# Roots of summed rows by ScalarE and VectorE instead of GpSimd, and tile 0's transposes inside the last product

## The chip, the cores and the metric

The kernel runs on one core of one Trainium2 chip. The metric is device time in microseconds (us) of one launch, as the median of several. Five engines of the core have a part: TensorE (PE; its weight loads are PEld), VectorE (DVE), ScalarE (ACT), GpSimd (POOL) and SyncE (SP), which issues most transfers. Each works through its own list of instructions in order; semaphores tie the lists together.

## The reference

Two blocks of a transformer, 512 tokens of width 1024, all in float32. What matters here is the seam between the second block's first layer (a gated MLP) and its second (attention in a sliding window):

```python
def rms_norm_2(x, g):
    y = xf * lax.rsqrt(jnp.mean(xf * xf, axis=-1, keepdims=True) + EPS)   # EPS = 1e-6
    return (y * g).astype(x.dtype)
...
y = gmlp_mixer(rms_norm_2(h, a_pre_g), ...)     # ends in  y @ w_out, 2048 -> 1024
h = h + rms_norm_2(y, a_post_g)                 # root "a", one per token
kv_in = rms_norm_2(h, kv_norm_g)                # root "h3", one per token
k_shared = kv_in @ w_k;  v_shared = kv_in @ w_v
...
q, z = jnp.split(rms_norm_2(h, b_pre_g) @ b_w_in, 2, axis=-1)   # same root "h3"
```

## The kernel before

Tokens lie in four tiles of 128 partitions. Every product is made of three passes of `fp32r` matmuls: each operand is split into a rounded part (`whi`, `actB_hi`) and a remainder (`wlo`, `actB_lo`), and `exact` adds hi*hi, hi*lo and lo*hi. The order of PE's work is a list of blocks made by `tensor_order`, which PE follows strictly; the other engines have their order written out by hand.

The output product of the gated layer comes as fourteen units `("a", n)` of two blocks each, `("A", n, r)` for two halves of rows; a block has four steps k of three matmuls. `rows_by_half` waits before each step for the half of `wlo` that it reads (`w7_lo`), so steps 2 and 3 of unit 13 wait for the second half of `lo_a(13)`. ScalarE writes the unit's `whi` (`hi_a`, L1155) and VectorE its `wlo` (`lo_a`, L1743).

Then, for each tile of tokens t:
- VectorE adds up the product (`add_kept`, L1849), ScalarE squares each half with a sum along the row (`square_a`, L950), VectorE multiplies by the gain (`part_gain`, L1895);
- GpSimd takes the root (`root`: L795 adds the two sums and EPS into `ms`, L798 raises it to -0.5 into `rstd`);
- VectorE adds it to the residual in two halves (`h3_in`, L1903), ScalarE squares these (`h3_out`), GpSimd takes the root of h3;
- ScalarE scales the tile (`normed_n`, L1304), PE transposes it (`turn("n", t)`, L2173, eight transposes in two banks), ScalarE copies it out as `actB_hi` (`turned_n`, L961), VectorE takes the remainder `actB_lo` (`rest_n`, L1421);
- PE makes the new layer's values (`("v5", t)`: eight steps, waits for both remainders of the tile) and keys (`("Fa", "k5", 0)` for tiles 0 and 1, `("Fa", "k5", 1)`, `("F", "k5", f)` for the rest).

GpSimd meanwhile splits the weights of v5, k5 and q5 (`split_half`: two `whi` at L841, then two `wlo` at L850, for each half). For k5 it waits until PE is done with unit 12, and for its second half until ScalarE has scaled it by the norm's gain (`scale_two`, L1313); for q5 until PE is done with unit 13. The roots stand in this list at places written in `after`: those of "a" for tiles 0 and 1 stand between the last two `v5lo`, the others among k5's and q5's splits. All the four tiles' roots, "a" and "h3", make eight of two instructions each.

The last lines of PE's order around the seam, before:

```python
o += [("A", n, r) for n in (range(4), range(4, 14))[half] for r in range(2)]
o += turn("n", 0) + turn("n", 1) + [("v5", 0), ("v5", 1)]
o += [("Fa", "k5", 0)] + turn("n", 2) + [("Fa", "k5", 1)] + turn("n", 3)
```

Of the kernel before, what the change touches and what calls it, by code (L numbers as in the profile page):

```python
# [8 lines left out]
P = 128  # L9
# [143 lines left out]
LANDED = landings()  # L153
SQUARES_A = [(0, 0), (1, 0), (2, 1), (3, 1), (0, 1), (1, 1), (2, 0), (3, 0)]
# [33 lines left out]
def tensor_order():  # L188
# [42 lines left out]
    o += turn("n", 0) + turn("n", 1) + [("v5", 0), ("v5", 1)]  # L231
# [87 lines left out]
def program(nc, x, p, pre_norm_gain, w_in, lambda_q1, lambda_k1, lambda_q2, lambda_k2, subln_gain,  # L319
# [9 lines left out]
    with ctx:  # L329
# [40 lines left out]
        mhalf = sb("mhalf", [P, 1])  # L370
# [141 lines left out]
        ms_ready = sem("ms_ready")  # L512
        rstd_ready = {n: sem(f"rstd_{n}") for n in NORMS}
# [4 lines left out]
        pads_made = sem("pads_made")  # L518
# [10 lines left out]
        msq_attn, rstd_attn, attn_normed, attn_out = (sem("msq_attn"), sem("rstd_attn"),  # L529
# [241 lines left out]
        def _(pool):  # L771
            pool.memset(ident[:, :], 0.0).then_inc(consts_made, 1)
            pool.memset(mhalf[:, :], -0.5).then_inc(consts_made, 1)
            pool.memset(ones[:, :], 1.0).then_inc(consts_made, 1)
            pool.wait_ge(consts_made, 3)
# [24 lines left out]
            def root_attn(h):  # L800
                pool.wait_ge(attn_sq, 4 * h + 4)
                pool.tensor_scalar(ms_attn[:, h, :], ss_attn[:, h, :], 1.0 / DV1, SUBLN_EPS, ALU.mult, ALU.add)\
                    .then_inc(msq_attn, 1)
                pool.wait_ge(msq_attn, h + 1)
                pool.tensor_tensor(r_attn[:, h, :], ms_attn[:, h, :], mhalf[:, 0:1].to_broadcast([P, T]), ALU.pow)\
                    .then_inc(rstd_attn, 1)
# [111 lines left out]
            after[at("v5", 0, 1) - 0.25] = [lambda: root("a", 0, D), lambda: root("a", 1, D)]  # L918
            after[at("v5", 0, 1)] = [lambda: root("h3", 0, D)]
            after[at("k5", 0, 0) - 0.5] = [lambda: root("h3", 1, D)]  # L920
            after[at("k5", 0, 1) - 0.5] = [lambda: root("a", 2, D)]
            after[at("k5", 0, 1)] = [lambda: root("a", 3, D), lambda: root("h3", 2, D)]
            after[at("q5", 0, 0) - 0.5] = [lambda: root("h3", 3, D)]
# [11 lines left out]
        def _(act):  # L935
# [67 lines left out]
            def job_out(i):  # L1003
# [7 lines left out]
                if s == "c":  # L1011
                    act.wait_ge(pads_made, 1)
# [222 lines left out]

            def h3_out(t):
                for c in range(2):
                    act.wait_ge(h3_ready, 2 * t + c + 1)
                    square("h3", t, c, resid[:, t, c * HALF:(c + 1) * HALF])
# [67 lines left out]
            def scale_two(s, h):  # L1307
# [3 lines left out]
                for k in range(4):  # L1311
                    w = src[:, k * 256:(k + 1) * 256]
                    A(w, w, ACT.Copy, scale=kvg[:, 4 * h + k:4 * h + k + 1]).then_inc(w_scaled, 1)  # L1313
# [11 lines left out]
            square_a(1, 0)  # L1325
            hi_a(10)
# [19 lines left out]
            h3_out(2)  # L1346
            normed_n(2)
            v5_out(0)
            h3_out(3)
# [57 lines left out]
        def _(dve):  # L1407
# [28 lines left out]
            V.memset(gcv[:, :, 0:2], 0.0).then_inc(pads_made, 1)  # L1436

            dve.wait_ge(consts_made, 5)
# [4 lines left out]
            V.memset(base1[0:64, HALF - 64:HALF], MASKED).then_inc(base_step, 1)  # L1443

# [460 lines left out]

            def rest_n(t):
                for j in range(2):
                    rest("n", t, j)
# [41 lines left out]
            h3_in(3)  # L1950
            v5_rest(0)
# [118 lines left out]
        def _(pe):  # L2070
# [105 lines left out]
            def ready(b):  # L2176
# [48 lines left out]
                if kind == "v5":  # L2225
                    pe.wait_ge(lo["n"], 2 * (s + 1))
# [30 lines left out]
            def work(b):  # L2257
# [64 lines left out]
                if kind == "v5":  # L2322
# [4 lines left out]
                    for k in range(KD):  # L2327
                        H, L = halves_of(n, k // 2)
# [29 lines left out]
            pe.wait_ge(consts_made, 4)  # L2358
# [29 lines left out]
```

## Time and profile before

| | |
|---|---|
| median of three runs | 885.3 us (885.14 to 886.25) |
| the profiled execution | 885.75 us, its span 884.0 us |
| PE busy | 868.2 us (98%), 4220 matmuls |
| VectorE, ScalarE, GpSimd busy | 537.2, 360.3, 542.8 us |

The span is the time from the first to the last instruction of the profile; what is left of the execution's time lies around it. Busy times are sums over instructions of an engine. PE's come from modelled ends of pipelined matmuls, so that what counts is where its next start is late. In the timelines an instruction that has been issued and waits for another engine's access counts as running: a duration above the usual one of its kind is such a wait.

### The profile page before, as it was taken

What the parts mean: (1) busy time and instruction counts of PE and PEld (TensorE: products, weight loads), DVE (VectorE), ACT (ScalarE), POOL (GpSimd) and SP (SyncE); (2) the same over time, 40 slices, a digit from 0 to 9 for tenths busy, and PEclk for the clock granted to TensorE, in tenths of its full rate; (3) what the DMA queues carried; (4) which work ended last, traced back from release to release, by engine and by line L of the source; (5) the groups of instructions that cost most, each with busy time, mean ns of one, the idle gap of its engine ahead of it and who ended that gap; (6) DMA issues with size and microseconds to landing.
All of it is one profiled execution on the core that took longest, in us unless ns stands there. A gap on an engine that the chain in (4) does not pass through costs nothing.

```text
span 884.0 us, 11936 instructions
## 1 busy us (share of the span) xinstructions
PE 868.2 (98%) x4220; PEld 722.0 (82%) x4220; DVE 537.2 (61%) x880; ACT 360.3 (41%) x804; POOL 542.8 (61%) x604
## 2 busy tenths in 40 slices
PE   8999999999999999999999999999997999999997
PEld 6888888888888787888888888888887888888886
DVE  6125648875035489775765535556996457788624
ACT  4123333431134377546112321113775536767622
POOL 7766556587789832317975038771359798566352
PEclk9999999999999999999999999999999999999999
DMA  7533231342322468885742253526962222112202
GB/s 198 167 120 96 74 92 51 96 143 92 128 90 96 124 146 177 208 203 190 162 124 95 73 190 96 125 90 152 217 180 71 72 73 93 51 49 72 73 1 95
DMA packets 81517, 102.65 MB, mean 116 GB/s; under 512 B 11826, under 2 KB 54322, under 8 KB 81459
## 3 DMA queue, kind: packets, MB, share of 16 engines
q1 hardware_dynamic: 72752, 85.12, 30.1%
q0 software_dynamic: 8704, 16.78, 11.2%
q8 instruction: 34, 0.56, 0.3%
q14 instruction: 25, 0.20, 0.1%
q10 hardware_dynamic: 2, 0.00, 0.0%
HBM read 99.79 MB, written 2.10 MB: 115 GB/s over the span
## 4 chain that ended last, share of the span: by engine, by line
PE 88%; POOL 4%; DVE 2%; DMA 2%; ACT 2%; issue 1%; POOLq 0%; DVEq 0%; ACTq 0%
PE bank L2076 26%; PE bank L2078 26%; PE bank L2077 26%; PE bank L2319 2%; PE bank L2347 1%; PE bank L2173 1%; DMA gain<-in_a_w_in 1%; DVE wlo L1667 1%; POOL wlo L850 1%; PE bank L2292 1%; PE bank L2342 1%; PE bank L2341 1%; DMA raw<-in_a_w_in 1%; POOL ms L795 1%; POOL whi L841 1%
## 5 line engine op out<-in xcount | busy, mean ns | idle before, releaser
L850 POOL TENSOR_TENSOR wlo<-raw,whi 128x512 fp32r<-128x512 f32 x204 | 280.4, 1404 | 0.7 <-ACT whi L972 0.7
L841 POOL TENSOR_SCALAR whi<-raw 128x512 fp32r<-128x512 f32 x202 | 140.8, 733 | 188.1 <-PE bank L2078 179.1
L2076 PE MATMUL bank<-actB_hi,whi 128*128 128x512 f32 (+1 forms) x416 | 159.6, 384 | 0.6 <-POOL wlo L850 0.6
L2077 PE MATMUL bank<-actB_lo,whi 128*128 128x512 f32 (+1 forms) x416 | 158.7, 381 | 0.0
L2078 PE MATMUL bank<-actB_hi,wlo 128*128 128x512 f32 (+1 forms) x416 | 158.5, 381 | 0.0
L2076 PE MATMUL bank<-whi,actA_hi 128*128 128x512 f32 x318 | 125.9, 396 | 1.2 <-DVE actA_lo L1421 0.7
L2078 PE MATMUL bank<-whi,actA_lo 128*128 128x512 f32 x318 | 124.0, 390 | 0.0
L2077 PE MATMUL bank<-wlo,actA_hi 128*128 128x512 f32 x318 | 123.9, 390 | 0.0
L2076 PEld LDWEIGHTS bank<-actB_hi,whi 128*128 128x128 f32 x416 | 78.3, 188 | 15.4 <-issue 1.1
L2078 PEld LDWEIGHTS bank<-actB_hi,wlo 128*128 128x128 f32 x416 | 78.2, 188 | 15.2
L2077 PEld LDWEIGHTS bank<-actB_lo,whi 128*128 128x128 f32 x416 | 78.3, 188 | 14.1
L2076 PE MATMUL bank<-actA_hi,whi 128*128 128x512 f32 x224 | 87.9, 392 | 0.0
L2077 PE MATMUL bank<-actA_lo,whi 128*128 128x512 f32 x224 | 87.4, 390 | 0.0
L2078 PE MATMUL bank<-actA_hi,wlo 128*128 128x512 f32 x224 | 87.3, 390 | 0.0
L2076 PEld LDWEIGHTS bank<-whi,actA_hi 128*128 128x128 f32 x318 | 59.7, 188 | 15.3 <-issue 1.9
L2078 PEld LDWEIGHTS bank<-whi,actA_lo 128*128 128x128 f32 x318 | 59.7, 188 | 12.6
L2077 PEld LDWEIGHTS bank<-wlo,actA_hi 128*128 128x128 f32 x318 | 59.8, 188 | 12.0 <-issue 0.2
L2076 PE MATMUL bank<-whi,actB_hi 128*128 128x512 f32 x144 | 56.5, 393 | 0.2 <-DVE wlo L1667 0.2
L2078 PE MATMUL bank<-whi,actB_lo 128*128 128x512 f32 x144 | 56.1, 390 | 0.0
L2077 PE MATMUL bank<-wlo,actB_hi 128*128 128x512 f32 x144 | 56.0, 389 | 0.0
L1776 DVE TENSOR_TENSOR acc<-acc,gcv 128x512 f32<-128x512 f32 x16 | 15.6, 974 | 58.3 <-ACT gcv L1228 58.3
L2078 PEld LDWEIGHTS bank<-actA_hi,wlo 128*128 128x128 f32 x224 | 42.1, 188 | 8.9
(269 smaller groups left out, 1579.4 us busy)
## 6 DMA issues: line engine op xcount, KB each, us to landing
raw<-in_a_w_in SPq DMA_DIRECT2D x44, 512.0 KB, 4.2
raw<-in_w_in SPq DMA_DIRECT2D x32, 512.0 KB, 3.9
raw<-in_b_w_in SPq DMA_DIRECT2D x16, 512.0 KB, 3.4
raw<-in_a_w_out SPq DMA_DIRECT2D x12, 512.0 KB, 3.3
gain<-in_a_w_out POOLq DMA_DIRECT2D x9, 512.0 KB, 8.2
raw<-in_w_out SPq DMA_DIRECT2D x8, 512.0 KB, 3.4
raw<-in_w_ple_gate SPq DMA_DIRECT2D x8, 512.0 KB, 3.3
gain<-in_a_w_in POOLq DMA_DIRECT2D x8, 512.0 KB, 7.7
```

Source lines behind the costliest of these rows:

```text
L795: pool.tensor_scalar(m, ss[:, n, t, 0:1], ss[:, n, t, 1:2], EPS, ALU.add, ALU.add).then_inc(ms_ready, 1)
L841: pool.tensor_scalar(H, src[:, i * HALF:(i + 1) * HALF], 1.0, 1.0, ALU.mult, ALU.mult).then_inc(w_hi, 1)
L850: ins = pool.tensor_tensor(L, src[:, i * HALF:(i + 1) * HALF], H.bitcast(f32), ALU.subtract)
L1667: V.tensor_tensor(L, src, H.bitcast(f32), ALU.subtract).then_inc(w7_lo, 1)
L1776: V.tensor_tensor(acc[:, f % 2, :], acc[:, f % 2, :], gcv[:, f % 2, 0:S], ALU.mult).then_inc(zu_made, 1)
L2076: M(out_, whi_, xhi_, start=start, stop=False)
L2077: M(out_, whi_, xlo_, start=False, stop=False)
L2078: return M(out_, wlo_, xhi_, start=False, stop=stop)
L2173: ins = nc.tensor.transpose(bank[:, k * P:(k + 1) * P], src, ident[:, :])
L2292: ins = M(bank[:, qt * P:(qt + 1) * P], wgtT1[:, k * P:(k + 1) * P], tile(vtok, k)[:, h * P:(h + 1) * P], start=k == 0, stop=k == qt)
L2319: ins = M(bank[:, n * P:(n + 1) * P], big[:, n, f * P:(f + 1) * P], wcT[:, (f // 2) * P:(f // 2 + 1) * P], start=True, stop=True)
L2341: M(out_, q, khi(g)[:, keys], start=True, stop=False)
```

## The change

1. The eight roots leave GpSimd. ScalarE now squares at a scale of 1/64 instead of 1/32, so that the sums are a quarter of the mean square. It adds a quarter of EPS to the first sum (`add_eps`, into `ms`) and takes the root of the sum of both (`std`, `Sqrt`, into `rstd`); this is half of the root mean square, with the table's error.
2. VectorE (`inverse`) makes one step of Heron of it and its reciprocal: four instructions on one column.
3. Tile 0's transposes stand ahead of the last block of the last product, `("A", 13, 1)`.
4. The first half of a v5 block waits for the first remainder of its tile only.
5. The lists of ScalarE and VectorE around the seam are rewritten. VectorE has tile 0's inverse and `h3_in(0)` ahead of the second half of `lo_a(13)`. ScalarE scales the second half of k5 in two parts, the second behind the squares of h3 of tile 0. A `Sqrt` of one column stands behind `square_a(1, 0)`, so that the table is loaded there.
6. Two semaphores are merged into others (`pads_made`, `msq_attn`), and GpSimd has one more memset at the start.

```diff
-    o += turn("n", 0) + turn("n", 1) + [("v5", 0), ("v5", 1)]
+    assert o.pop() == ("A", 13, 1)
+    o += turn("n", 0) + [("A", 13, 1)] + turn("n", 1) + [("v5", 0), ("v5", 1)]
...
+            pool.memset(eps[:, :], EPS / 4).then_inc(consts_made, 1)
             pool.memset(ones[:, :], 1.0).then_inc(consts_made, 1)
-            pool.wait_ge(consts_made, 3)
+            pool.wait_ge(consts_made, 4)
...
-            after[at("v5", 0, 1) - 0.25] = [lambda: root("a", 0, D), lambda: root("a", 1, D)]
-            after[at("v5", 0, 1)] = [lambda: root("h3", 0, D)]
-            after[at("k5", 0, 0) - 0.5] = [lambda: root("h3", 1, D)]
-            after[at("k5", 0, 1) - 0.5] = [lambda: root("a", 2, D)]
-            after[at("k5", 0, 1)] = [lambda: root("a", 3, D), lambda: root("h3", 2, D)]
-            after[at("q5", 0, 0) - 0.5] = [lambda: root("h3", 3, D)]
...
-                A(junk[:, :], src, ACT.Square, scale=1.0 / 32, accum_out=ss[:, NORMS[name], t, c:c + 1])\
+                A(junk[:, :], src, ACT.Square, scale=1.0 / 64 if name in BY_ROOT else 1.0 / 32,
+                  accum_out=ss[:, NORMS[name], t, c:c + 1])\
...
+            def add_eps(name, t, tiles, c, done):
+                n = NORMS[name]
+                act.wait_ge(squared[name], done)
+                A(ms[:, n, t:t + tiles], ss[:, n, t:t + tiles, c], ACT.Identity, bias=eps[:, 0:1]).then_inc(std_step, 1)
+            def std(name, t, c, done):
+                n = NORMS[name]
+                act.wait_ge(std_step, STD_STEP["eps", name, t // 2 * 2 if name == "a" else t])
+                act.wait_ge(squared[name], done)
+                A(rstd[:, n, t:t + 1], ss[:, n, t, c:c + 1], ACT.Sqrt, bias=ms[:, n, t:t + 1]).then_inc(std_step, 1)
...
             square_a(1, 0)
+            act.wait_ge(consts_made, 6)
+            A(lams[:, 7:8], eps[:, 0:1], ACT.Sqrt)
...
             hi_a(13)
+            add_eps("a", 0, 2, 0, 2)
             square_a(0, 1)
+            std("a", 0, 1, 5)
             square_a(1, 1)
-            scale_two("k5", 1)
+            std("a", 1, 1, 6)
+            scale_two("k5", 1, (0, 1))
+            add_eps("a", 2, 2, 1, 4)
             h3_out(0)
+            scale_two("k5", 1, (2, 3))
+            normed_n(0)
             h3_out(1)
-            normed_n(0)
+            turned("n", 0, 0)
             normed_n(1)
-            turned_n(0)
+            turned("n", 0, 1)
             square_a(2, 0)
+            std("a", 2, 0, 7)
             turned_n(1)
             square_a(3, 0)
+            std("a", 3, 0, 8)
             h3_out(2)
+            h3_square(3, 0)
             normed_n(2)
             v5_out(0)
-            h3_out(3)
+            h3_square(3, 1)
+            h3_std(3)
             v5_out(1)
             normed_n(3)
...
+            def inverse(name, t):
+                n, c = NORMS[name], ROOTED_LAST[name, t]
+                nth = 3 * next(inverses)
+                last, mean, first, sum_ = (ss[:, n, t, k:k + 1] for k in (c, 1 - c, 2, 3))
+                root = rstd[:, n, t:t + 1]
+                dve.wait_ge(std_step, STD_STEP[name, t])
+                V.tensor_tensor(mean, last, ms[:, n, t:t + 1], ALU.add).then_inc(root_step, 1)
+                V.reciprocal(first, root).then_inc(root_step, 1)
+                dve.wait_ge(root_step, nth + 2)
+                V.scalar_tensor_tensor(sum_, mean, first, root, ALU.mult, ALU.add).then_inc(root_step, 1)
+                dve.wait_ge(root_step, nth + 3)
+                V.reciprocal(root, sum_).then_inc(rstd_ready[name], 1)
...
             lo_a(13, (0,))
             part_gain(0, 1)
+            inverse("a", 0)
+            h3_in(0)
             lo_a(13, (1,))
             part_gain(1, 1)
-            h3_in(0)
+            inverse("a", 1)
+            inverse("h3", 0)
             h3_in(1)
             add_kept(6, 0, p03_kept(0), a_out_(2, 0), (c7_made, 28 + 6))
+            inverse("h3", 1)
+            rest("n", 0, 0)
+            rest("n", 0, 1)
             add_kept(6, 1, p03_kept(1), a_out_(3, 0), (c7_made, 28 + 10))
-            rest_n(0)
             part_gain(2, 0)
-            rest_n(1)
+            inverse("a", 2)
+            rest("n", 1, 0)
             h3_in(2)
+            rest("n", 1, 1)
             part_gain(3, 0)
+            inverse("a", 3)
+            inverse("h3", 2)
             h3_in(3)
+            inverse("h3", 3)
...
-                    pe.wait_ge(lo["n"], 2 * (s + 1))
+                    pe.wait_ge(lo["n"], 2 * s + 1)
...
                     for k in range(KD):
+                        if k == 4:
+                            pe.wait_ge(lo["n"], 2 * t + 2)
```

## Rows read from the trace of the kernel before

**Rows 1.** The page's chain; busy us (count) by engine, granted clock, DMA, one stretch.
```profile
PE 88%; POOL 4%; DVE 2%; DMA 2%; ACT 2%; issue 1%; POOLq 0%; DVEq 0%; ACTq 0%
...
666.74:688.00 21.26, 15.93 (x128) 14.96 (x128) 11.59 (x17) 13.34 (x28) 20.27 (x29) 1.00 0.06 21
```

**Rows 2.** PE's waits, 640 to 712 us: total, times, longest.
```profile
PE bank L2173 <- ACT big L1304: 4.0, 4, 1.7
...
PE bank L2076 <- issue: 1.4, 2, 0.7
```

**Rows 3.** PE's timeline: start, us, line, operation [idle before, what ended it].
```profile
662.49 0.39 PE L2076 MATMUL bank<-whi,actA_hi 128*128 128x512 f32 x1
...
666.35 0.39 PE L2078 MATMUL bank<-whi,actA_lo 128*128 128x512 f32 x1
...
668.46 1.06 PE L2173 MATMUL bank<-ident,big 128*128 128x128 f32 x8 [1.72 <-ACT big L1304]
...
670.33 1.07 PE L2173 MATMUL bank<-ident,big 128*128 128x128 f32 x8 [0.81 <-ACT big L1304]
...
672.09 0.36 PE L2076 MATMUL bank<-v5hi,actB_hi 128*128 128x256 f32 x1 [0.69 <-issue]
...
682.15 1.06 PE L2173 MATMUL bank<-ident,big 128*128 128x128 f32 x8 [1.25 <-ACT big L1304]
...
688.07 0.36 PE L2076 MATMUL bank<-v5hi,actB_hi 128*128 128x256 f32 x1 [0.70 <-issue]
...
711.24 0.47 PE L2076 MATMUL bank<-actB_hi,whi 128*128 128x512 f32 x1 [0.59 <-POOL wlo L850]
```

**Rows 4.** ScalarE's timeline, 639 to 668 us.
```profile
639.57 1.06 ACT L1155 ACTIVATE whi<-raw 128x1024 fp32r<-128x1024 f32 x1 [2.00 <-PE bank L2078]
...
662.85 0.63 ACT L950 ACTIVATE junk<-resid 128x512 f32<-128x512 f32 x1 [1.65 <-DVE resid L1903]
...
667.18 1.13 ACT L1304 ACTIVATE big<-resid,rstd 128x1024 f32<-128x1024 f32 x1
```

**Rows 5.** The timelines of VectorE, then of GpSimd (POOL), 654 to 666 us.
```profile
655.90 1.09 DVE L1895 TENSOR_TENSOR big<-big,gain 128x512 f32<-128x512 f32 x1
...
658.11 1.70 DVE L1743 TENSOR_TENSOR wlo<-raw,whi 128x1024 fp32r<-128x1024 f32 x1
...
659.74 0.68 DVE L1895 TENSOR_TENSOR big<-big,gain 128x512 f32<-128x512 f32 x1
...
660.34 1.21 DVE L1743 TENSOR_TENSOR wlo<-raw,whi 128x1024 fp32r<-128x1024 f32 x1
...
662.08 0.74 DVE L1903 SCALAR_TENSOR_TENSOR resid<-big,rstd,resid 128x512 f32<-128x512 f32 x1
...
663.92 1.78 DVE L1903 SCALAR_TENSOR_TENSOR resid<-big,rstd,resid 128x512 f32<-128x512 f32 x1 [0.44 <-POOL rstd L798]
...
654.77 1.69 POOL L841 TENSOR_SCALAR v5hi<-raw 128x512 fp32r<-128x512 f32 x1 [1.01 <-ACT raw L1313]
...
657.44 1.29 POOL L850 TENSOR_TENSOR v5lo<-raw,v5hi 128x512 fp32r<-128x512 f32 x1
...
658.89 1.62 POOL L795 TENSOR_SCALAR ms<-ss 128x1 f32<-128x1 f32 x1 [0.16 <-ACT junk L950]
...
663.87 1.29 POOL L850 TENSOR_TENSOR v5lo<-raw,v5hi 128x512 fp32r<-128x512 f32 x1
```

**Rows 6.** By line: least/median/most ns of one, first and last start, forms.
```profile
L1983 DVE TENSOR_TENSOR den<-rs,esk x16: 144/162/1250, 717.8 to 834.8; 128x4 f32<-128x4 f32 x16
...
L1395 ACT ACTIVATE esk<-den x16: 187/188/190, 717.5 to 834.6; 128x4 f32<-128x4 f32 x16
...
L1358 ACT ACT_TABLE_LOAD  x1: 1283/1283/1283, 702.2 to 702.2; - x1
...
L841 POOL TENSOR_SCALAR whi<-tok x4: 610/614/1043, 666.8 to 672.0; 128x512 fp32r<-128x512 f32 x4
...
L1421 DVE TENSOR_TENSOR actB_lo<-bank,actB_hi x16: 674/681/691, 320.4 to 688.5; 128x512 fp32r<-128x512 f32 x16
```

More of the change, by code:

```diff
@@ L153 @@
 LANDED = landings()
+STD_STEP = {step: n + 1 for n, step in enumerate(
+    [("eps", "a", 0), ("a", 0), ("a", 1), ("eps", "a", 2), ("eps", "h3", 0), ("h3", 0), ("eps", "h3", 1), ("h3", 1),
+     ("a", 2), ("a", 3), ("eps", "h3", 2), ("h3", 2), ("eps", "h3", 3), ("h3", 3)])}
+ROOTED_LAST = {("a", t): int(t < 2) for t in range(4)} | {("h3", t): 1 for t in range(4)}
 SQUARES_A = [(0, 0), (1, 0), (2, 1), (3, 1), (0, 1), (1, 1), (2, 0), (3, 0)]
@@ L369, in program @@
         rstd = sb("rstd", [P, 8, T])
-        mhalf = sb("mhalf", [P, 1])
+        mhalf, eps = sb("mhalf", [P, 1]), sb("eps", [P, 1])
         prob3 = sb("prob3", [P, D])
@@ L512, in program @@
         ms_ready = sem("ms_ready")
+        std_step, root_step = sem("std_step"), sem("root_step")
+        BY_ROOT = ("a", "h3")
         rstd_ready = {n: sem(f"rstd_{n}") for n in NORMS}
@@ L517, in program @@
         consts_made, ws_masked = sem("consts_made"), sem("ws_masked")
-        pads_made = sem("pads_made")
         base_step, lam_step, lam_exp, cols_scaled = (sem("base_step"), sem("lam_step"), sem("lam_exp"),
@@ L528, in program @@
         wt_copied, attn_copied, attn_sq = sem("wt_copied"), sem("attn_copied"), sem("attn_sq")
-        msq_attn, rstd_attn, attn_normed, attn_out = (sem("msq_attn"), sem("rstd_attn"),
+        rstd_attn, attn_normed, attn_out = (sem("rstd_attn"),
                                                       sem("attn_normed"), sem("attn_out"))
@@ L802, in root_attn @@
                 pool.tensor_scalar(ms_attn[:, h, :], ss_attn[:, h, :], 1.0 / DV1, SUBLN_EPS, ALU.mult, ALU.add)\
-                    .then_inc(msq_attn, 1)
-                pool.wait_ge(msq_attn, h + 1)
+                    .then_inc(ms_ready, 1)
+                pool.wait_ge(ms_ready, next(roots))
                 pool.tensor_tensor(r_attn[:, h, :], ms_attn[:, h, :], mhalf[:, 0:1].to_broadcast([P, T]), ALU.pow)\
@@ L1011, in job_out @@
                 if s == "c":
-                    act.wait_ge(pads_made, 1)
+                    act.wait_ge(base_step, 4)
                     if f >= 2:
@@ L1234, in square_a, with h3_square, h3_std @@
                 square("a", t, c, a_out_(t, c))
+            def add_eps(name, t, tiles, c, done):
[7 more added lines that the diff above has]
+                A(rstd[:, n, t:t + 1], ss[:, n, t, c:c + 1], ACT.Sqrt, bias=ms[:, n, t:t + 1]).then_inc(std_step, 1)
+            def h3_square(t, c):
+                act.wait_ge(h3_ready, 2 * t + c + 1)
+                square("h3", t, c, resid[:, t, c * HALF:(c + 1) * HALF])
+            def h3_std(t):
+                add_eps("h3", t, 1, 0, 2 * t + 1)
+                std("h3", t, 1, 2 * t + 2)
             def h3_out(t):
-                for c in range(2):
-                    act.wait_ge(h3_ready, 2 * t + c + 1)
-                    square("h3", t, c, resid[:, t, c * HALF:(c + 1) * HALF])
+                h3_square(t, 0)
+                h3_square(t, 1)
+                h3_std(t)
             def y4_hi(j):
@@ L1305, in normed_n, with scale_two @@
                   scale=rstd[:, NORMS["h3"], t:t + 1]).then_inc(tok_ready["n"], 1)
-            def scale_two(s, h):
+            def scale_two(s, h, cols=range(4)):
                 src, landed, value = raw_of(UNIT_NO[s, 0], h)
@@ L1310, in scale_two @@
                 act.wait_ge(small_in, 16 * 13)
-                for k in range(4):
+                for k in cols:
                     w = src[:, k * 256:(k + 1) * 256]
@@ L1434, in normed @@
                 ins.then_inc(tok_ready[turn], 1)
-            V.memset(gcv[:, :, 0:2], 0.0).then_inc(pads_made, 1)
-            dve.wait_ge(consts_made, 5)
+            dve.wait_ge(consts_made, 6)
             V.tensor_copy(base1, iot).then_inc(base_step, 1)
@@ L1443, in _ @@
             V.memset(base1[0:64, HALF - 64:HALF], MASKED).then_inc(base_step, 1)
+            V.memset(gcv[:, :, 0:2], 0.0).then_inc(base_step, 1)
             def square_x(t):
@@ L1904, in h3_in @@
                                            resid[:, t, half], ALU.mult, ALU.add).then_inc(h3_ready, 1)
+            inverses = count(0)
+            def inverse(name, t):
[10 more added lines that the diff above has]
+                V.reciprocal(root, sum_).then_inc(rstd_ready[name], 1)
             def rest_n(t):
@@ L2356, in work @@
                     return ins
-            pe.wait_ge(consts_made, 4)
+            pe.wait_ge(consts_made, 5)
             for b in ORDER:
```

## The prediction

> **What bounds the kernel now.** I read the page first: PE carries 88% of the chain that ended last, and nothing else more than 4% [rows 1], so the change can only take away time in which PE stands still, or make more of it. The table of stretches then shows where: from 666.74, where the gated layer's last product ends, to 688.00 PE is busy 15.93 of 21.26 us, at a granted clock of 1.00 [rows 1]. PE's waits over this stretch are 4.0 us for ScalarE's normed tiles, in four, and 1.4 that the list puts down to issue, in two [rows 2]. PE's timeline places them [rows 3]: the last product's last matmul starts at 666.35 and takes 0.39; tile 0's transposes start at 668.46 (1.72 idle), tile 1's at 670.33 (0.81), the first v5 product at 672.09 (0.69: it waits for VectorE's second remainder of tile 0), tile 2's transposes at 682.15 (1.25), the third v5 block at 688.07 (0.70, in the same way). With the little that is left at tile 3 that is the 5.3 us of the stretch, 0.6% of the span, and all that the change can win.
>
> **What makes the tiles late.** I read the other engines' timelines beside each other [rows 4, 5]. In the kernel before, GpSimd's root of tile 0's sum begins at 658.89 and needs 1.62 us for its first step, on one column, because VectorE works on two operands in SBUF in the meantime. That is the pattern of the whole stretch: such a VectorE instruction and a GpSimd one never overlap, and when both queue they alternate. VectorE's wlo at 658.11 takes 1.70 instead of 1.21, behind GpSimd's v5lo, which ends at 658.73. GpSimd's v5hi at 654.77 takes 1.69 instead of 0.61, behind a wlo, and VectorE's product at 655.90, issued behind that, takes 1.09 instead of 0.68. A half of h3 takes 1.78 instead of 0.74 beside a v5lo of 1.29 [rows 5, 6]. VectorE instructions with one operand in PSUM (the remainders, 0.68) keep their time.
>
> **Part by part.**
> Removed from GpSimd: eight roots of two instructions. The two of tiles 0 and 1 stood between the two v5lo and pushed the second one from 658.7 to 663.87 [rows 5]. Without them it is queued at 658.7, and k5's four instructions (two whi of 0.61, two wlo of 1.29) follow as soon as PE is done with unit 12, at 661.3: from unit 13's third step at 662.49 to its last matmul at 666.35 there are 17 pitches of 0.227 [rows 3], so its first step starts six pitches ahead of 662.49, at 661.1, and unit 12's last matmul ends 0.16 behind that. GpSimd's load is the same; it comes earlier, into the stretch where VectorE has its dependent work.
>
> Added to ScalarE: six additions and eight roots of one column. The nearest row is an exponential of 128x4, 0.19 [rows 6]; the next larger one, a square of 128x512, is 0.63 [rows 4], so each lies between 0.1 (overlapped) and 0.63, and I take 0.2. One load of the table, 1.28 [rows 6], plus 0.2 goes into ScalarE's idle 2.00 us before 639.57 [rows 4]: nothing. Were that idle time missing it would delay whi of the tenth unit by 1.5.
>
> Added to VectorE: 8 x 4 instructions of one column. The nearest row is 0.16 each [rows 6]; with 0.2 from one to the next that depends on it, a root costs 0.7. Two of the four (the sum, and the Heron step) have two operands in SBUF. Their price is the disputed term. The row of a 128x4 sum of two SBUF tiles has 144, 162 and 1250 ns as least, median and most, so a small one can wait for a whole GpSimd instruction: 0 to 1.1 more each. I let them wait.
>
> Moved: tile 0's eight transposes (0.9) ahead of the last block of the last product, and on VectorE the root and both halves of h3 of tile 0 ahead of the second half of wlo of the last unit. PE needs that half from 662.49, in the middle of the block before the transposes [rows 3]; before, it was there at 661.55 [rows 5]. A wait there stops everything behind it on PE.
>
> The start: one more memset of one column on GpSimd, below 0.1, ahead of an ident that PE has until the gain lands. I cost it at nothing.
>
> **The sum, walked through.** VectorE: first half of wlo ends 659.8, as before. GpSimd's second v5lo then runs to 661.0; the product with the gain, issued at 659.74, ends 661.5 (before: 660.42). Tile 0's inverse takes to 662.3. Its first half of h3 ends 663.2; GpSimd's first k5 wlo runs to 664.4; the second half ends 665.0; the second k5 wlo runs to 666.15; only then does wlo's second half run, to 667.2. PE waits for it from 662.5 to 667.3: **4.8 us**. PE ends that block (6 matmuls, pitch 0.227) at 668.7.
> ScalarE has the root of tile 0's h3 at 666.2 and then lets k5's second half go (at 667.0), so that GpSimd has two whi and two wlo from 667.7 to 671.4. VectorE's gain product, tile 1's inverse and tile 0's second inverse fall among them and end at 671.6 (without waits of the small ones: 669.0). The normed tile takes 1.14 [rows 4]: 672.8. Transposes start at 672.9 instead of behind the product: **4.2 us idle**. They end at 673.8, the last block (2.7) at 676.5, tile 1's transposes at 677.6. There the first v5 block starts, against 672.09: 5.5 us late.
> The rest: v5's second block wants tile 1's second remainder, which now stands behind tile 2's h3 on VectorE, and waits 2.6 in two places; tile 2's transposes wait 2.9, since all the small ones and h3 of tiles 2 and 3 run among GpSimd's q5 work. The third v5 block starts at about 696.3, against 688.07: **+8.2 us**. Behind it PE is bound by itself until 711.24, and its 0.59 there is GpSimd working from PE's own release, so it shifts along. The walk has three places where two engines ask within 0.1 us; won the other way they give back up to 1.6. So 6.6 to 8.6, middle **7.5**.
> The profiled execution took 885.75, its span 884.0 and 1.75 around it; it would become 893.3. The median of the runs is 885.3, 0.45 less: 892.8.
> The same bookkeeping, applied to the kernel before, gives tile 0's normed tile at 668.4 (trace: 668.31) and PE's transposes of tile 2 at 682.3 (682.15). That is why I trust its waits.
>
> A rule that bears on the disputed term: the Trainium skill, "SBUF — State Buffer", section "Who interferes with whom", says that a VectorE instruction with two SBUF inputs and a GpSimd instruction that reads SBUF exclude each other for the whole instruction, whichever came first. It makes no exception for small ones. The trace agrees for the large (1.78 against 0.74) and, in its maximum, for the small. By the page the small ones pay, which is the sum above; without it they might not, which is the first rival.
>
> **Rivals.**
> *Small sums slip through.* Only the large instructions alternate with GpSimd. For it: the median of 162 ns; against it: the maximum of 1250. PE still waits 4.8 at the last unit's second half, then 1.6 for tile 0 and 1.8 for tile 1, but the tail is short (1.4 in v5's second block, 0.4 at tile 2): the third v5 block at about 691.2, +3.0 us, 888.3.
> *The engines miss each other; faster.* If GpSimd's instructions fall into VectorE's pauses, VectorE goes through undelayed: wlo's second half at 663.1 (PE waits 0.7), tile 0's normed tile at 666.1 (1.6), 0.2 at tile 1, 0.4 in v5's second block, nothing at tiles 2 and 3. That is 2.9 idle instead of 5.3, 2.4 less; with the v5 blocks started on the first half of a tile the walk comes to 3.8 less. So 881.5 to 882.9, say 882.3. For it: this is what one gets by adding durations alone, and one collision decides much: if the second v5lo waits behind h3 rather than ahead of the gain product, VectorE gets its 1.25 back. It decides when wlo's second half ends before about 664.3. Against it: every time the two queued in the rows, they alternated.
> *A wash.* Half of the collisions: 885.3, within 0.2%.
> *PE loses its clock.* The granted clock is 1.00 in the stretch [rows 1], but no idle there exceeds 1.72; a wait of 4.8 has no row. If the level fell from 2.4 to 1.2 GHz behind it, each us of matmuls at that level would cost another. I put this into the upper end. The Trainium skill, "TensorE: Matmul & The Clock Gate", section "What's actually happening", says that an idle PE falls to the lower level; no row of this trace shows it.
> *The square is not in the root's table.* Then each of 8 roots would cost two loads of 1.28 on ScalarE, some 20 us, most of it on the path: 900 or more. Against it: the trace loads a table three times in all (the row of one is in [rows 6]), though squares, copies, tanh, gelu and exponentials mix.
>
> **How the numbers follow.** Full collisions 0.45; large ones only 0.23; faster 0.20; wash 0.09; tables 0.03. The range 883.5 to 895.0 takes in the middle cases and leaves out most of the faster one and the tables, about 2 in 10. 0.2% (1.8 us) is about what a measurement of this kernel can tell from no change. Faster 0.20, same 0.09, slower 0.71. The likeliest case alone: 891.9 to 893.9.
>
> **What would show it.** Right: a wait of PE on VectorE's wlo inside the last unit's first block, 4 us or more; the second v5lo straight behind the first; h3's halves at 0.74 and 1.8 in turn; small VectorE sums above 1 us at times; tile 0's transposes after 670. Wrong: wlo's second half done by 664; GpSimd idle while VectorE is busy; or a granted clock below 1.00, or tables loaded more than four times.

## The result and the profile after

| | before | after |
|---|---|---|
| median of the runs | 885.78 us (885.14 to 886.25, 5 runs) | 892.84 us (892.36 to 894.29, 5 runs) |
| the profiled execution, its span | 885.75, 884.0 us | 892.84, 891.1 us |
| PE busy | 868.2 us | 871.4 us |
| VectorE, ScalarE, GpSimd busy | 537.2, 360.3, 542.8 us | 550.3, 365.8, 536.2 us |

The changed kernel is slower: ratio 1.0085, 95% interval 1.007 to 1.010. The forecast was 892.8. The time is the one predicted, but not all of the steps are, as the parts below show.

The page's chain, and PE's waits from 640 to 722 us (total, times, longest) in the changed kernel. They answer to [rows 1, 2]:

```profile
PE 89%; DVE 6%; issue 1%; POOL 1%; ACT 1%; DMA 1%; DVEq 0%; POOLq 0%; ACTq 0%
```

```profile
PE bank L2138 <- DVE wlo L1779: 4.5, 1, 4.5
PE bank L2235 <- ACT big L1329: 4.2, 2, 2.7
PE bank L2138 <- DVE actB_lo L1458: 0.8, 1, 0.8
PE bank L2138 <- POOL wlo L859: 0.6, 1, 0.6
PE bank L2138 <- issue: 0.3, 1, 0.3
```

VectorE's part of the chain went from 2% to 6%, and a wait of 4.5 us on `wlo` (L1779, the line that was L1743) is new. PE's timeline places the waits (start, us, line, operation, idle before; L2138 to L2140 are the matmuls, L2235 the transposes):

```profile
661.76 0.39 PE L2140 MATMUL bank<-whi,actA_lo 128*128 128x512 f32 x1
666.63 0.80 PE L2138 MATMUL bank<-whi,actA_hi 128*128 128x512 f32 x1 [4.48 <-DVE wlo L1779]
667.22 0.63 PE L2139 MATMUL bank<-wlo,actA_hi 128*128 128x512 f32 x1
667.65 0.63 PE L2140 MATMUL bank<-whi,actA_lo 128*128 128x512 f32 x1
...
672.25 1.94 PE L2235 MATMUL bank<-ident,big 128*128 128x128 f32 x8 [2.69 <-ACT big L1329]
673.84 0.78 PE L2138 MATMUL bank<-whi,actA_hi 128*128 128x512 f32 x1
...
677.80 1.04 PE L2235 MATMUL bank<-ident,big 128*128 128x128 f32 x8
678.59 0.37 PE L2138 MATMUL bank<-v5hi,actB_hi 128*128 128x256 f32 x1
...
684.36 0.39 PE L2138 MATMUL bank<-v5hi,actB_hi 128*128 128x256 f32 x1 [0.76 <-DVE actB_lo L1458]
...
690.44 1.06 PE L2235 MATMUL bank<-ident,big 128*128 128x128 f32 x8 [1.51 <-ACT big L1329]
...
695.01 0.36 PE L2138 MATMUL bank<-v5hi,actB_hi 128*128 128x256 f32 x1
```

Two things are to be seen. First, PE stands still twice, for 4.48 and 2.69 us, where the kernel before had 1.72 and 0.81 [rows 3]. Second, the matmul at 667.65 starts 0.43 behind the one at 667.22; ahead of the wait that distance was 0.23. The stretches say why (busy us and count by engine, then the granted clock, DMA share, GB/s):

```profile
661.00:666.00 5.00, 1.15 (x6) 0.61 (x4) 4.91 (x5) 2.29 (x8) 4.49 (x4) 1.00 0.18 62
666.00:671.00 5.00, 2.93 (x6) 1.83 (x6) 4.86 (x11) 0.48 (x3) 4.48 (x5) 0.50 0.65 213
671.00:676.00 5.00, 3.75 (x13) 3.40 (x14) 3.39 (x8) 4.61 (x10) 2.39 (x4) 0.50 0.29 102
676.00:681.00 5.00, 5.00 (x36) 4.55 (x36) 3.66 (x6) 3.33 (x9) 2.88 (x4) 0.98 0.00 0
```

Behind the wait of 4.48 us the granted clock is 0.50, that is 1.2 GHz instead of 2.4, for about ten us (666 to 676), while VectorE is busy for 4.86 of 5.00 us and PE for 2.93.

Where the time went is read best from starts, counted from the place of the wait, unit 13's third step. The matmul ahead of it starts at 661.76, so that step would have started at 661.99; in the kernel before it started at 662.49.

| start, us from the third step's place | before | after | later by |
|---|---|---|---|
| the third step itself | 0 | 4.64 | 4.6 |
| tile 0's transposes | 5.97 | 10.26 | 4.3 |
| first v5 product | 9.60 | 16.60 | 7.0 |
| tile 2's transposes | 19.66 | 28.45 | 8.8 |
| third v5 block | 25.58 | 33.02 | 7.4 |

These 7.4 us are the loss in this stretch. The place itself stands 0.5 us earlier in the changed kernel's trace, so the third v5 block starts 6.9 later on the clock of the trace; the two profiled executions differ by 7.1.

VectorE's timeline shows what PE waited for, and GpSimd's what was beside it:

```profile
657.42 1.71 DVE L1779 TENSOR_TENSOR wlo<-raw,whi 128x1024 fp32r<-128x1024 f32 x1
659.06 1.78 DVE L1931 TENSOR_TENSOR big<-big,gain 128x512 f32<-128x512 f32 x1
...
661.81 2.56 DVE L1939 SCALAR_TENSOR_TENSOR resid<-big,rstd,resid 128x512 f32<-128x512 f32 x2
664.29 2.28 DVE L1779 TENSOR_TENSOR wlo<-raw,whi 128x1024 fp32r<-128x1024 f32 x1
...
668.36 1.15 DVE L1951 TENSOR_TENSOR ss<-ss,ms 128x1 f32<-128x1 f32 x1
...
669.61 1.11 DVE L1954 SCALAR_TENSOR_TENSOR ss<-ss,rstd 128x1 f32<-128x1 f32 x1
```

```profile
656.75 3.54 POOL L859 TENSOR_TENSOR v5lo<-raw,v5hi 128x512 fp32r<-128x512 f32 x2
660.95 1.20 POOL L850 TENSOR_SCALAR whi<-tok 128x512 fp32r<-128x512 f32 x2 [0.66 <-PE bank L2140]
662.12 3.37 POOL L859 TENSOR_TENSOR wlo<-tok,whi 128x512 fp32r<-128x512 f32 x2
```

The second `v5lo` stands straight behind the first (x2, 3.54 us), where two roots and 5.1 us stood between them before [rows 5]. So the product with the gain takes 1.78 where it took 0.68, and the second half of `wlo` 2.28 where it took 1.21. Two sums of one column take 1.15 and 1.11 us.

### The profile page after: what moved, and what is told of

The parts are those of the page before. It is cut to its first block, busy times and chain, and to the rows that moved or that the text cites. A ratio compares the mean times of both kernels' runs of the same rounds, so it can differ in the third digit from the quotient of the medians.

```text
span 891.1 us, 11978 instructions
## 1 busy us (share of the span) xinstructions
PE 871.4 (98%) x4220; PEld 724.5 (81%) x4220; DVE 550.3 (62%) x912; ACT 365.8 (41%) x820; POOL 536.2 (60%) x589
## 4 chain that ended last, share of the span: by engine, by line
PE 89%; DVE 6%; issue 1%; POOL 1%; ACT 1%; DMA 1%; DVEq 0%; POOLq 0%; ACTq 0%
PE bank L2138 27%; PE bank L2139 26%; PE bank L2140 26%; PE bank L2235 2%; PE bank L2381 2%; PE bank L2411 1%; PE bank L2354 1%; PE bank L2406 1%; DVE wlo L1779 1%; PE bank L2405 1%; DVE wlo L1703 1%; DMA raw<-in_a_w_in 1%; DVE big L1931 1%; DVE resid L1939 1%; PE bank L2345 1%
## 5 line engine op out<-in xcount | busy, mean ns | idle before, releaser
L2138 PE MATMUL bank<-actB_hi,whi 128*128 128x512 f32 (+1 forms) x416 | 159.6, 384 | 0.6 <-POOL wlo L859 0.6
L2140 PE MATMUL bank<-actB_hi,wlo 128*128 128x512 f32 (+1 forms) x416 | 158.5, 381 | 0.0
L2138 PE MATMUL bank<-whi,actA_hi 128*128 128x512 f32 x318 | 126.9, 399 | 5.4 <-DVE wlo L1779 4.5
L2140 PE MATMUL bank<-whi,actA_lo 128*128 128x512 f32 x318 | 124.7, 392 | 0.0
L2138 PEld LDWEIGHTS bank<-actB_hi,whi 128*128 128x128 f32 x416 | 78.3, 188 | 15.5 <-issue 1.0
L2140 PEld LDWEIGHTS bank<-actB_hi,wlo 128*128 128x128 f32 x416 | 78.2, 188 | 15.3
L2138 PE MATMUL bank<-actA_hi,whi 128*128 128x512 f32 x224 | 87.9, 392 | 0.0
L2140 PE MATMUL bank<-actA_hi,wlo 128*128 128x512 f32 x224 | 87.3, 390 | 0.0
L2138 PEld LDWEIGHTS bank<-whi,actA_hi 128*128 128x128 f32 x318 | 60.3, 190 | 19.5 <-DVE wlo L1779 4.9
L2140 PEld LDWEIGHTS bank<-whi,actA_lo 128*128 128x128 f32 x318 | 60.3, 189 | 12.8
L2138 PE MATMUL bank<-whi,actB_hi 128*128 128x512 f32 x144 | 56.5, 393 | 0.2 <-DVE wlo L1703 0.2
L2140 PE MATMUL bank<-whi,actB_lo 128*128 128x512 f32 x144 | 56.1, 390 | 0.0
L2140 PEld LDWEIGHTS bank<-actA_hi,wlo 128*128 128x128 f32 x224 | 42.0, 188 | 8.8
```

What stands on the lines that cost most here:

```text
L2138: M(out_, whi_, xhi_, start=start, stop=False)
L2140: return M(out_, wlo_, xhi_, start=False, stop=stop)
```

## The experiments

All were timed against the kernel before on their own chip; its medians there were 885.7 to 885.8.

A median holds more than this stretch. The place of unit 13's third step is at 661.99 us in the trace of the changed kernel and at 663.74 in that of the second experiment's kernel, which differs from it in nothing ahead of 660 us; by so much single executions differ ahead of the seam. So each trace is also read by its stretch, the time from that place to the start of the third v5 block: 25.6 us in the kernel before, 33.0 in the changed one.

### The halves of wlo first

```diff
-            inverse("a", 0)
-            h3_in(0)
-            lo_a(13, (1,))
+            lo_a(13, (1,))
+            inverse("a", 0)
+            h3_in(0)
```

> The changed kernel with one line moved: VectorE makes the second half of wlo of the last unit ahead of tile 0's inverse and h3, as the kernel before does. My theory (the time lies in VectorE and GpSimd taking turns, and the order only decides where PE meets it): PE's wait of 4.5 us in the last unit's first block goes down to about 0.2, but tile 0's transposes then wait 6 us or more, since the chain of tile 0 gets that instruction ahead of it instead; the total falls by about 1, to 892 us. Rival (the order is the cause): the 4.5 us are won, with the lost clock behind them 6 or more: 886 to 888 us.

Measured: 891.87 us (891.3 to 894.18), ratio 1.0074, interval 1.0059 to 1.0089. The stretch is 31.2. The wait on `wlo` is gone, and where the changed kernel waits 4.48 and then 2.69 us, this one waits once, at the next place:

```profile
670.61 1.94 PE L2235 MATMUL bank<-ident,big 128*128 128x128 f32 x8 [6.12 <-ACT big L1329]
```

The order on VectorE places the wait and doesn't make it: what is short is VectorE's time up to tile 0's normed rows. The theory held: it had 892 us and 6 us or more at this place.

### The two sums in another form of instruction

```diff
-                V.tensor_tensor(mean, last, ms[:, n, t:t + 1], ALU.add).then_inc(root_step, 1)
+                V.tensor_scalar(mean, last, ms[:, n, t:t + 1], None, ALU.add).then_inc(root_step, 1)
...
-                V.scalar_tensor_tensor(sum_, mean, first, root, ALU.mult, ALU.add).then_inc(root_step, 1)
+                V.tensor_scalar(sum_, mean, first, root, ALU.mult, ALU.add).then_inc(root_step, 1)
```

The second and third operands are here scalars read through a pointer, one for each partition, and no longer tensors. The arithmetic is the same.

> The changed kernel with the two small VectorE instructions of each inverse that read two tensors in SBUF written as instructions that read one tensor and take the other operands as scalars of the partition; the arithmetic is the same. My theory (a small instruction waits for GpSimd's because of its second tensor operand): they stay at 0.15 to 0.2 us each, PE's first wait stays near 4.5, tile 0's normed tile comes about 2.5 us sooner, and the waits at tiles 1 and 2 and in the second v5 block shrink; 3 to 5 us less in all, 888 to 890 us. Rival (every VectorE instruction can be held, or the scalar operands are read in the same way): they still show 0.5 to 1.2 us, and the time stays at 892 to 893.

Measured: 890.22 us (889.77 to 891.03), ratio 1.0052, interval 1.0037 to 1.0067; the stretch is 29.5. The two lines by group (total us, mean ns), first in the changed kernel, then here:

```profile
L1954 DVE SCALAR_TENSOR_TENSOR ss<-ss,rstd 128x1 f32<-128x1 f32 x8 | 4.5, 558 | 0.3
...
L1951 DVE TENSOR_TENSOR ss<-ss,ms 128x1 f32<-128x1 f32 x8 | 3.5, 432 | 2.4 <-ACT rstd L1251 2.4
```

```profile
L1954 DVE TENSOR_SCALAR ss<-ss,rstd 128x1 f32<-128x1 f32 x8 | 2.2, 273 | 0.3
...
L1951 DVE TENSOR_SCALAR ss<-ss,ms 128x1 f32<-128x1 f32 x8 | 1.6, 203 | 2.2 <-ACT rstd L1251 2.2
```

In the new form none of the sixteen waits (the longest of each line took 0.22 and 0.28 us); PE's waits for normed tiles fell from 4.2 to 1.9 us, the one on `wlo` stayed at 4.5, and so did the lower clock behind it (0.55 in 666 to 671). So the small sums are worth 2.6 of the 7.1 us, by the stretch 3.5 of 7.4. The mechanism held; the median is just above the 888 to 890 that I expected.

### GpSimd held back

GpSimd waits, ahead of its second `v5lo`, until tile 0's second root is there:

```diff
+            after.setdefault(at("v5", 0, 1) - 0.25, []).append(lambda: pool.wait_ge(rstd_ready["h3"], 1))
```

> The changed kernel with GpSimd held: its second v5lo, and all that stands behind it, waits until tile 0's root of h3 is done. Nothing else differs. My theory (GpSimd's work having moved ahead into VectorE's dependent stretch is the cause): PE's first wait falls from 4.5 to about 1.2 us, tile 0's normed tile is there at about 666.0 instead of 672.1, the clock stays at 1.00, and the total falls by 3.5 to 5.5 us, to 887.5 to 889.5, though GpSimd's work now meets tiles 1 and 2. Rival (the added instructions on VectorE and ScalarE are themselves the cost): the first wait stays above 3 us and the time within 1 of 892.8, or longer for GpSimd's being late.

Measured: 889.98 us (889.69 to 891.44), ratio 1.0051, interval 1.0036 to 1.0066, just above the expectation; the stretch is 29.0. The wait on `wlo` falls to 0.75 and the clock stays at 1.00; tile 0's sums take 0.15 and 0.22.

```profile
663.82 0.50 PE L2139 MATMUL bank<-whi,actA_hi 128*128 128x512 f32 x1 [0.75 <-DVE wlo L1780]
```

```profile
679.92 1.25 DVE L1952 TENSOR_TENSOR ss<-ss,ms 128x1 f32<-128x1 f32 x1
```

But the collisions move on: tile 1 has small sums of 1.03 and 1.12 us, tile 3 of 1.25, 1.14 and 1.24, and PE waits 6.9 us for normed tiles, in four. GpSimd's early work on v5 and k5 makes the first wait; the small sums are a second cause by themselves.

### The clock kept up

Matmuls that no one reads (`ones` by `ident`, into a free bank) stand where PE waits: 36 ahead of the third step of unit 13, 20 ahead of tile 0's transposes.

```diff
+            def fill(count):
+                pe.wait_ge(c7_made, 28 + 14)
+                for _ in range(count):
+                    M(psum[7][:, 0:P], ident[:, :], ones[:, :], start=True, stop=True)
...
+                    if (n, r, k) == (13, 0, 2):
+                        fill(36)
...
+                        if (name, t, j) == ("n", 0, 0):
+                            fill(20)
```

> The changed kernel with 36 small matmuls into a free bank in the place where PE waits for the second half of wlo, and 20 more where it waits for tile 0's normed tile; they take less time than the waits. It asks what the lower granted clock costs, 0.50 from 666 to 676 us in the changed kernel. My theory: the clock stays at 1.00, the transposes take 1.06 instead of 1.94 and the last product's matmuls come 0.23 apart instead of 0.43; of the 3.3 us of slow work 1.2 lie in the second wait anyway, so about 2 us less, 890.8. Rival (the clock's loss is hidden in the waits behind it): the same time, 892.8.

Measured: 895.71 us (894.92 to 897.9), ratio 1.0118. The expectation was missed because of my size for the filling:

```profile
663.27 8.20 PE L2228 MATMUL bank<-ones,ident 128*128 128x128 f32 x72
...
672.68 4.62 PE L2228 MATMUL bank<-ones,ident 128*128 128x128 f32 x40
```

A product of two float32 tiles of 128x128 counts as two matmuls, so 36 took 8.20 us and outlasted the wait. The next kernel has 18 and 14 of them.

> As e4_warm, but with 18 and 14 small matmuls. In e4_warm one such matmul on float32 took the time of two (36 of them 8.2 us, 0.23 each), so that they outlasted the waits and pushed the kernel to 895.7 us; these take 4.1 and 3.2 us, less than the waits of the changed kernel (4.5, and 2.7 plus 1.3 that slow matmuls fill). My theory: the clock stays at 1.00 and the time falls by about 2 us, to 890.8. Rival (the clock's loss is hidden elsewhere): 892.8.

Measured: 894.91 us (893.49 to 896.36), ratio 1.0109, interval 1.0094 to 1.0125. Its timeline:

```profile
662.30 4.18 PE L2228 MATMUL bank<-ones,ident 128*128 128x128 f32 x36
666.96 0.50 PE L2138 MATMUL bank<-whi,actA_hi 128*128 128x512 f32 x1 [0.47 <-DVE wlo L1779]
...
668.45 3.29 PE L2228 MATMUL bank<-ones,ident 128*128 128x128 f32 x28
672.48 1.09 PE L2242 MATMUL bank<-ident,big 128*128 128x128 f32 x8 [0.75 <-ACT big L1329]
...
682.02 0.36 PE L2138 MATMUL bank<-v5hi,actB_hi 128*128 128x256 f32 x1 [1.72 <-issue]
...
691.33 1.06 PE L2242 MATMUL bank<-ident,big 128*128 128x128 f32 x8 [2.64 <-ACT big L1329]
```

The clock is 1.00 throughout, the transposes take 1.09 instead of 1.94, and tile 1's start at 676.42 instead of 677.80. Then PE waits 1.72 and 2.64 us where it waited 0.28 and 1.51: tile 1's v5 block starts at 682.02, against 681.93, and tile 2's transposes at 691.33, against 690.44. What the full clock gives is gone by the next wait: the others set the end. So the theory's 890.8 failed, but the rival's 892.8 isn't met either. The four executions lie in two pairs: 893.5 and 893.8 with a mean granted clock of 1.00, 896.1 and 896.4 with 0.995 and 0.996, in which the filling did not keep the clock throughout. The profiled one, with its clock whole, is still 0.9 us slower than the changed kernel. Why is left open: the filling ends within a us of what PE waits for and may move PE's requests for the next buffers; no run here takes that apart.

### Tile 0's transposes alone

The kernel before, with only the new order on PE:

```diff
-    o += turn("n", 0) + turn("n", 1) + [("v5", 0), ("v5", 1)]
+    assert o.pop() == ("A", 13, 1)
+    o += turn("n", 0) + [("A", 13, 1)] + turn("n", 1) + [("v5", 0), ("v5", 1)]
```

> The kernel before with one part of the change alone: tile 0's transposes ahead of the last block of the last product. Roots stay on GpSimd, the lists of VectorE and ScalarE as before. The normed tile comes at 668.3 as before, so PE waits 4.6 us ahead of the last block instead of 1.7 behind it. By the walk that is a mere exchange (the block then fills the other waits): 885.7 if the clock holds; with the clock lost for some 10 us as in the changed kernel, 0.9 for the transposes and 2.4 for the block more, 887.5 to 889. Rival (moving the transposes up is a gain in itself): under 885.

Measured: 887.44 us (886.11 to 888.74, 10 runs), ratio 1.0019, interval 1.0010 to 1.0028; the profiled execution is its fastest, 886.11, with a stretch of 26.4.

```profile
667.76 1.84 PE L2174 MATMUL bank<-ident,big 128*128 128x128 f32 x8 [4.19 <-ACT big L1305]
```

The normed tile is no earlier, so PE waits for it with the product unissued behind it, and the clock falls (0.69 in 666 to 671). This part alone costs 1.6 us by the median, just below the 887.5 to 889 expected for a lost clock. The executions differ with the clock: the three with the lowest mean granted clock (0.994) took 888.1 to 888.3, the three with the highest (0.997 and 0.998) 886.1 to 886.9.

### The v5 blocks on one half alone

The kernel before, with the first half of a v5 block waiting for the first remainder only:

```diff
-                    pe.wait_ge(lo["n"], 2 * (s + 1))
+                    pe.wait_ge(lo["n"], 2 * s + 1)
...
                     for k in range(KD):
+                        if k == 4:
+                            pe.wait_ge(lo["n"], 2 * t + 2)
```

> The kernel before with another part alone: a v5 block starts on the first remainder of its tile and waits for the second at its fifth step. Two waits of 0.7 us lose 0.6 each, but tile 2's normed tile is bound by GpSimd's roots and comes when it came, so that the first 0.6 is given back there: 0.6 us less in all, 885.1. Rival (both are won): 1.2 us less, 884.5.

Measured: 885.02 us (884.55 to 886.12, 11 runs; before 885.83), ratio 0.9994, interval 0.9985 to 1.0002. The stretch is 24.8. The waits of 0.7 of [rows 3] are gone, and 0.6 of these 1.4 us comes back at tile 2 (1.83 instead of 1.25) and tile 3 (0.28 instead of 0.23). It is the only part for which the runs lean to a gain, and it isn't clear of noise.

### Both causes away

The changed kernel with the sums in the second form, and GpSimd held until the second half of `wlo` is there:

```diff
+            after.setdefault(at("v5", 0, 1) - 0.25, []).append(lambda: pool.wait_ge(w7_lo, 2 * TWO_NO[UNIT_NO["a", 13]] + 2))
```

> The changed kernel with both causes taken away: the two small instructions of each inverse read one tensor each (as e2_small), and GpSimd's second v5lo, with k5's and q5's work behind it, waits until VectorE has made the last unit's second half of wlo. My theory: PE waits about 1.1 there, 1.6 at tile 0, under 1 in each later place, the clock stays at 1.00, and the kernel is 1.5 to 2.7 us faster than the kernel before: 883.0 to 884.2. Rival (e2 and e3 won the same microseconds, or the later tiles are bound by something else): 886 to 889.

Measured: 886.05 us (885.55 to 887.83, 11 runs), ratio 1.0005, interval 0.9997 to 1.0014. Against the changed kernel's 892.84 this is 6.8 us back of 7.1. The two causes together account for nearly the whole loss. Alone they gave 2.6 and 2.9 by the medians; by the stretch they gave 3.5 and 4.0 of 7.4, and together 7.7, so there the two add up. Parts 3 to 6 of the change are still in this kernel, so together they cost nothing that shows. The gain over the kernel before that I forecast (883.0 to 884.2) didn't come; the time is in the rival's range. PE's waits:

```profile
PE bank L2236 <- ACT big L1330: 3.1, 3, 1.6
PE bank L2139 <- DVE wlo L1780: 0.9, 1, 0.9
PE bank L2139 <- issue: 0.7, 1, 0.7
PE bank L2139 <- POOL wlo L859: 0.6, 1, 0.6
PE bank L2139 <- DVE actB_lo L1459: 0.4, 1, 0.4
```

Without the 0.6 outside the stretch these are 5.1 us, against 5.3 before, and the stretch is 25.3 against 25.6. (This profiled execution took 887.51, 1.5 above the median; unit 13's third step had its place at 664.31, 1.8 later than before, so that time was lost ahead of the stretch.) GpSimd stood still 5.05 us in its hold, and the kernel is no slower than before for it:

```profile
665.35 1.68 POOL L859 TENSOR_TENSOR v5lo<-raw,v5hi 128x512 fp32r<-128x512 f32 x1 [5.05 <-DVE wlo L1780]
```

### The roots alone

The changed kernel with PE's order, the place of `wlo`'s second half and the v5 waits as before:

```diff
-    assert o.pop() == ("A", 13, 1)
-    o += turn("n", 0) + [("A", 13, 1)] + turn("n", 1) + [("v5", 0), ("v5", 1)]
+    o += turn("n", 0) + turn("n", 1) + [("v5", 0), ("v5", 1)]
...
+            lo_a(13, (1,))
             inverse("a", 0)
             h3_in(0)
-            lo_a(13, (1,))
...
-                    pe.wait_ge(lo["n"], 2 * s + 1)
+                    pe.wait_ge(lo["n"], 2 * (s + 1))
...
                     for k in range(KD):
-                        if k == 4:
-                            pe.wait_ge(lo["n"], 2 * t + 2)
```

> The changed kernel with three of its edits undone: tile 0's transposes stand behind the last product again, wlo's second half is made ahead of the roots, and v5 waits for both halves of a remainder. What is left is the roots' route over ScalarE's Sqrt and VectorE's step of Heron, with GpSimd's list shortened by them. Theory (the loss comes from the roots' small VectorE instructions and from VectorE's large ones taking turns with GpSimd's): the time stays at the changed kernel's, 892 (891 to 893.5), with a wait of 3 us or more ahead of tile 0's transposes and small sums of about 1 us each. Rival (the transposes' place inside the product was a large share of the loss): 888 to 890, with the granted clock at 1.00 in 666 to 671.

Measured: 893.99 us (893.23 to 894.05), ratio 1.0091, interval 1.0078 to 1.0105, half a us above the theory's band.

```profile
671.22 1.94 PE L2234 MATMUL bank<-ident,big 128*128 128x128 f32 x8 [3.46 <-ACT big L1328]
676.05 1.94 PE L2234 MATMUL bank<-ident,big 128*128 128x128 f32 x8 [2.89 <-ACT big L1328]
```

The roots' new route, with the lists of ScalarE and VectorE that go with it, makes the whole loss: 8.2 us by the median, against 7.1 for the changed kernel, with intervals that overlap (1.0078 to 1.0105, 1.0070 to 1.0100), and a stretch of 32.8 against 33.0. That the other parts give anything back isn't shown. The rival, with the transposes' place as a large share, fell. Where [rows 3] had 1.72 and 0.81, both waits on normed tiles are about 3 us, and the clock is 0.50 from 671 to 681.

### Tile 0's transposes once more

The kernel without both causes, with the transposes behind the last product again:

```diff
-    assert o.pop() == ("A", 13, 1)
-    o += turn("n", 0) + [("A", 13, 1)] + turn("n", 1) + [("v5", 0), ("v5", 1)]
+    o += turn("n", 0) + turn("n", 1) + [("v5", 0), ("v5", 1)]
```

> The kernel with the second instruction form of the two sums and GpSimd's hold until the last wlo half is written, and tile 0's transposes moved behind the last product again. Theory (once the two causes are gone, the place of the transposes is worth what their wait of 1.60 us shows): the wait ahead of tile 0's transposes goes below 0.3 us, some of it comes back at tile 1 (which then follows without a product between), and the time is 885.2 (884.5 to 886.5). Rival (VectorE and GpSimd behind it set the end, whatever TensorE's order is): 886.0 to 887, no gain over the same kernel with the transposes inside.

Measured: 885.86 us (885.32 to 886.39, 11 runs), ratio 1.0002, interval 0.9993 to 1.0011. PE's timeline at tiles 0 and 1:

```profile
668.14 1.03 PE L2235 MATMUL bank<-ident,big 128*128 128x128 f32 x8
671.18 1.86 PE L2235 MATMUL bank<-ident,big 128*128 128x128 f32 x8 [2.00 <-ACT big L1329]
```

Tile 0's transposes wait for nothing, as the theory had it, but tile 1's wait 2.00 us, more than the 1.60 that went. The granted clock is 0.57 from 671 to 673. The time lies inside the theory's band and 0.14 below the rival's, and can't be told from that of the kernel with the transposes inside (886.05; stretches 25.7 and 25.3): the order moves the wait by a tile and does no more that shows, so this run decides nothing about the rival.

## Why the prediction was right, and where only its sum was

- **The first wait, 4.8 us.** Right: 4.48, or 4.64 by starts, for the reason given: the second `v5lo` queued straight behind the first, the product with the gain at 1.78, h3's halves and `wlo`'s second half between k5's instructions. The hold removed it down to 0.75.
- **The small sums wait for GpSimd.** Right as a mechanism, and mis-sized. I let both of every root wait, up to 1.1 each; eight of each kind took 432 and 558 ns in the mean, against 203 and 273 in the form that never waits, 4.1 us more in all. Their share of the time is 2.6 us. The first rival, in which they slip through, gave 888.3; the run in which they do gave 890.2 (by the stretch +3.9, against +3.0 walked). That case had no lower clock in it, and the trace has 0.55 from 666 to 671.
- **The second wait, 4.2 us.** Too large: 2.69. The lower clock stands in part of its place. At 1.2 GHz PE's six matmuls ahead of it took 0.2 more each, 1.2 us, in which the normed tile came nearer. Tile 0's transposes came at +4.3 instead of the walked +4.4.
- **The clock.** This is the step that failed. I put its loss only in the upper end, since no idle in the stretch was longer than 1.72 us. It fell to 0.50 behind the 4.48 and added 12 x 0.2 for matmuls and 0.9 for transposes, 3.3 us of PE's time that my sum had at nothing. The Trainium skill, "TensorE: Matmul & The Clock Gate", section "What's actually happening", says that an idle PE goes to the lower of the levels; this trace agrees, with 0.50. The Trainium skill, "TensorE: Matmul & The Clock Gate", section "Wait — 56ns, not 53.3ns?", gives a start-to-start time of 426.7 ns for a matmul of 512 columns at that level; the 0.43 us read above agrees.
- **The tail, +2.7 us behind the first v5 product.** Too large: +0.4 (from 7.0 to 7.4). PE arrived there 1.5 us later than walked (7.0 against 5.5), and the others used that time. The second kernel with the clock kept up shows the exchange: PE is sooner by 1.4 us at tile 1's transposes, and the tail's waits grow from 0.28 and 1.51 to 1.72 and 2.64. So two errors, no clock loss in the sum and too long a tail, cancelled. That the walk's 8.2, or its middle of 7.5, came so near to the measured 7.1 to 7.4 is in part luck.
- **ScalarE.** A small `Identity` or `Sqrt` took 0.28 and 0.30, not 0.2. The Trainium skill, "ScalarE: Activation LUTs", section "What ACT_TABLE_LOAD costs", gives about 280 ns for an instruction of one column whose bias is read through a pointer; the trace agrees, and the row that I took, an exponential of 0.19, was the wrong neighbour. The table load cost nothing on the path, as said: it stood in ScalarE's idle time at 637.09, and 0.48 us of idle were left behind it.

```profile
637.09 1.28 ACT L1352 ACT_TABLE_LOAD   x1
638.38 0.20 ACT L1352 ACTIVATE lams<-eps 128x1 f32<-128x1 f32 x1
639.07 2.01 ACT L1159 ACTIVATE whi<-raw 128x1024 fp32r<-128x1024 f32 x2 [0.48 <-PE bank L2140]
```

- **The faster case.** It needed `wlo`'s second half before 664.3; it ended at 666.57. In the kernel without both causes PE's third step is only 1.0 us late (665.33, where the matmul ahead of it starts at 664.08), near the 0.7 of that case, and the time is still not below that of before. That case, 882.3, was too good even with the two causes away. The trace shows where: the case had 0.4 us of waits behind the first v5 block, and the trace has 0.68, 0.38 and 1.29. There GpSimd, whose work the hold moved on, is busy for 9.9 of 10 us (671 to 681), and VectorE's product with the gain takes 1.63 us again. So large instructions still take turns in the tail. What the roots' chain over two engines adds (0.30 on ScalarE, then 0.8 in four instructions on VectorE) was not tested.

## What to carry to other kernels

GpSimd's roots went to VectorE, whose dependent work PE waits for, and which was already busy for 10.6 of the 11 us from 655 to 666 in the kernel before. Such a move can cost more than the steps' own time: it also lets the relieved engine run ahead and take the shared access at the busiest moment. Ask what the relieved engine will do with its time, and hold it back if nobody wants its result yet. Give small instructions on VectorE a form with one tensor operand and the rest as pointer scalars where GpSimd is busy. And where a new wait of several us stands before PE, price the matmuls behind it at half the clock, but look whether the next wait swallows that.

## What the runs showed of the hardware

- A VectorE instruction of one column with two tensors in SBUF can wait for a whole GpSimd instruction: it took 0.15 or 0.22 us while GpSimd was held, and up to 1.25 beside it. The same arithmetic with pointer scalars, which also lie in SBUF, took 0.20 and 0.27 us sixteen times of sixteen. The Trainium skill, "SBUF — State Buffer", section "Who interferes with whom", speaks of two SBUF inputs; the runs show that a pointer scalar isn't one of them.
- The clock's fall doesn't follow from the length of one wait. Behind waits of 4.48, 4.19 and 3.46 us it was 0.50 to 0.69; behind 2.00 us in the last kernel it was 0.57, and tile 1's transposes took 1.86 us, while waits of 2.28 and 2.64 us with GpSimd held, and 1.72 before, left it at 1.00.
- A float32 product of 128x128 tiles is two matmuls in the records, 0.23 us together at full clock (8.20 us for 36).
